# Moving the sixteen-bit split of a transposed tile from ScalarE to VectorE, and sharing its joining between the two

## The chip, the cores and the metric

The kernel runs on one core of a Trainium2 chip. The metric is the device time of one execution in microseconds. The core's engines run side by side, each with its own instruction stream: TensorE (PE, matmuls, its weight loads shown apart as PEld), VectorE (DVE), ScalarE (ACT), GpSimd (POOL) and SyncE (SP), whose queue issues most of the DMA. They wait for one another only through semaphores.

## The reference

One layer of a hybrid attention block over 256 tokens and 2048 features, in fp32, cut here to its steps:

```
h    = rms_norm(x, norm_gain)
proj = h @ w_in                       # 9,296 columns: q, k, v, gate of A; q, k, v, gate of B; indexer q, k, w
A    = chunked attention, 8 heads of 128, with a clipped relative-position bias
B    = attention over the top 64 keys of an indexer, 8 heads of 128, with a distance penalty
y    = concat(A * silu(gate_A), B * silu(gate_B))
x    = x + y @ w_out
out  = rms_norm(x, final_gain)
```

Both attentions end in a softmax whose probabilities are multiplied by the values. For that product TensorE needs the probabilities turned, keys on partitions and queries along the free axis. The change is about this turning.

## The kernel before, in words

**Blocks and units.** The weights stream through in blocks of 512 columns, each in 8 units of 512 KB. For every unit SP loads a raw slot; ScalarE copies it to a reduced-precision format (`split_hi`, L710); VectorE subtracts that from the raw slot (`split_lo`, L1013); TensorE runs the unit's matmuls with both parts (`feature_unit`, L486 and L490, or `unit`, L455 to L457). The ring has 4 slots. So `split_hi` of unit c waits until TensorE has finished unit c - 4, and SP's load of a slot waits until VectorE has split the one before in it. In the code `split_hi(g, c)` with c from 8 to 13 means unit c - 8 of the next block.

**Pairs of heads.** Blocks 10 to 17 bring in, beside their own columns, one pair of heads each: blocks 10 to 13 the four pairs of B (`feature_attention`), blocks 14 to 17 those of A (`gate_block`). TensorE computes a pair's scores after unit 1 of its block (`score_pair`) and its product with the values after unit 0 of the next (`value_pair`, first matmul L642). Between the two, written out by hand on each engine, among the splits of units 6 to 13:

- VectorE adds the bias, takes the maxima, and after ScalarE's exponentials (`exps`) scales the probabilities by the inverse sums (`normalise`, L1361 and L1365), then goes on with `split_lo` 6.
- ScalarE, after `split_hi` 6 and `features_low`, makes the planes (`planes_out`, L880): the fp32 probabilities, 768 words for each partition, are read as 1536 sixteen-bit numbers, all low halves written first and all high halves behind them.
- SP issues one DMA transpose of the sixteen-bit planes (`turn_planes`, L355), between its loads of units 1 and 2 of the next block.
- ScalarE, after `split_hi` 9 and (where there is a next pair) `stage_q`, joins the turned planes to words again (`pT_out`, L884), then copies 512 of the words in reduced precision to `pT_hi` (L886).
- VectorE subtracts that to give `pT_lo` (`pT_rest`, L1371), behind `split_lo` 9 and `stage_rest`. `value_pair` waits for it.

In the gate blocks VectorE also scales the gate (`gate_out`, L1402), ScalarE takes its tanh (`tanh_gate`, L920, ahead of `split_hi` 8), and VectorE multiplies (`gated`, L1411 and L1414).

**The end of the pairs.** After the last pair's `pT_out` and `split_hi` 10, ScalarE copies the gated outputs in reduced precision (`y_hi`, L950); VectorE, after `pT_rest` and `split_lo` 10, subtracts (`y_lo`, L1442). The output projection (L455) waits for one `y_lo` ahead of each unit.

Of the kernel before, what the change touches and what calls it, by code (L numbers as in the profile page):

```python
# [57 lines left out]
def hybrid_block(nc, xT, x, norm_gain, w_blocks, w_narrow, rel_bias, wo_blocks, final_gain, out):  # L58
# [4 lines left out]
    ACT = mybir.ActivationFunctionType  # L63
# [3 lines left out]
    with ExitStack() as ctx:  # L67
        def sb(name, shape, dt=f32):
            return ctx.enter_context(nc.sbuf_tensor(name, shape, dt))
# [4 lines left out]
        def sem(name):  # L74
            return ctx.enter_context(nc.semaphore(name))
# [26 lines left out]
        probs_T = sb("probs_T", [P, 2, P + T])  # L102
# [24 lines left out]
        probs = sb("probs", [P, 2, P + T])  # L127
# [96 lines left out]
        normed = sem("normed")  # L224
        planes_made = sem("planes_made")
        planes_turned = sem("planes_turned")
        words_made = sem("words_made")
        pt_hi_done = sem("pt_hi_done")
        pt_lo_done = sem("pt_lo_done")
        pv_done = sem("pv_done")  # L230
# [24 lines left out]
        def flat(t):  # L255
            return t.rearrange("p a b -> p (a b)")
# [23 lines left out]
        planes = flat(qiT[:, :, :]).bitcast(u16)[:, 0:2 * WORDS].rearrange("p (s n) -> p s n", s=2)  # L280
        planes_T = flat(qiT[:, :, :]).bitcast(u16)[:, 2 * WORDS:4 * WORDS].rearrange("p (s n) -> p s n", s=2)

        def halves(words):
            return flat(words[:, :, :]).bitcast(u16).rearrange("p (n s) -> p s n", s=2)
# [417 lines left out]
        def _(act):  # L702
            def split_hi(g, c):

                u = c % UNITS
                s = u % RING
                act.wait_ge(w_landed[s], g * (16 * UNITS // RING) + 16 * (c // RING + 1))
                if not (isinstance(g, int) and g * UNITS + c < RING):
                    act.wait_ge(mm_done, g * UNITS + (c - RING + 1))
                nc.scalar.activation(hi_slots[:, s, 0:UK * CB], w_raw[:, s, :], ACT.Copy).then_inc(hi_done, 1)  # L710
# [15 lines left out]
            def features_low(g, half, early, n=T):  # L726

                pair = half
                act.wait_ge(mm_done, g * UNITS + (4 * half + 4))
                if not (isinstance(g, int) and g == G_QI):  # L730
                    act.wait_ge(feat_out, feature_use(g, half, early) - 1)
                parts = acc[:, 2 * pair * CB:2 * pair * CB + 2 * CB].rearrange("p (f c) -> p f c", f=2)
                nc.scalar.activation(low[:, half, :, 0:n], parts[:, :, n:2 * n], ACT.Copy).then_inc(low_out, 1)  # L733
# [131 lines left out]
            def exps(pair, rated):  # L865
                for t, p in enumerate((p1, p0)):
                    act.wait_ge(max_done, 2 * pair + (t + 1))
                    for h in range(2):
                        if rated:
                            last = nc.scalar.activation(p[:, h, :], p[:, h, :], ACT.Exp, bias=neg_top[:, t, h:h + 1],  # L870
                                                        scale=q_rate[:, 1 - t:2 - t], accum_out=p_sum[:, t, h:h + 1])
                        else:
                            last = nc.scalar.activation(p[:, h, :], p[:, h, :], ACT.Exp, bias=neg_max[:, t, h:h + 1],  # L873
                                                        accum_out=p_sum[:, t, h:h + 1])
                last.then_inc(exp_done, 1)

            def planes_out(pair):

                act.wait_ge(normed, pair + 1)
                nc.scalar.activation(planes, halves(probs), ACT.Copy).then_inc(planes_made, 1)  # L880

            def pT_out(pair):
                act.wait_ge(planes_turned, 16 * pair + 16)
                nc.scalar.activation(halves(probs_T), planes_T, ACT.Copy).then_inc(words_made, 1)  # L884
                act.wait_ge(words_made, pair + 1)
                nc.scalar.activation(pT_hi.rearrange("p (h t) -> p h t", h=2), pT0,  # L886
                                     ACT.Copy).then_inc(pt_hi_done, 1)

            def output(pair):

                act.wait_ge(pv_done, pair + 1)
                nc.scalar.activation(o_flat[:, ds(pair * 2 * T, 2 * T)], aux[3][:, :], ACT.Copy,
                                     scale=0.5).then_inc(aux_read[3], 1)

            def feature_attention(g, i, q_next, k_next, keys):
                exps(i, True)
                split_hi(g, 6)
                features_low(g, 0, 0)
                planes_out(i)
                split_hi(g, 7)  # L900
                split_hi(g, 8)
                split_hi(g, 9)
                stage_q(q_next, k_next, keys)
                pT_out(i)
                split_hi(g, 10)
                features_low(g, 1, 0)
                split_hi(g, 11)
                split_hi(g, 12)
                output(i)
                split_hi(g, 13)  # L910
# [11 lines left out]
            def gate_block(g, i, q_next):  # L922
                exps(i + 4, False)
                split_hi(g, 6)
                features_low(g, 0, 0)
                planes_out(i + 4)
                split_hi(g, 7)
                tanh_gate(i, 0)
                split_hi(g, 8)
                split_hi(g, 9)  # L930
                if q_next is not None:
                    stage_q(q_next, q_next + 4, 8)
                pT_out(i + 4)
                split_hi(g, 10)
# [73 lines left out]
        def _(dve):  # L1008
            def split_lo(g, c):

                s = c % RING
                dve.wait_ge(hi_done, g * UNITS + (c + 1))
                nc.vector.tensor_tensor(lo_slots[:, s, 0:UK * CB], w_raw[:, s, :], hi_slots[:, s, 0:UK * CB].bitcast(f32),  # L1013
                                        ALU.subtract).then_inc(lo_done, 1)
# [33 lines left out]
            def qk_chunk(c):  # L1048
                return qk[:, ds(c, 1), :].rearrange("p o (f t) -> p (o f) t", f=2)
# [245 lines left out]
            def stage_rest(q_chunk, k_chunk, pair):  # L1295

                q_tile = qk[:, ds(q_chunk, 1), :].rearrange("p o (h t) -> p (o h) t", h=2)
                k_tile = qk[:, ds(k_chunk, 1), :].rearrange("p o (h t) -> p (o h) t", h=2)
                dve.wait_ge(q_staged, pair + 1)
                nc.vector.tensor_tensor(q_lo, q_tile[:, :, P:T], q_hi.bitcast(f32), ALU.subtract)  # L1300
                nc.vector.tensor_tensor(k_lo, k_tile, k_hi.bitcast(f32), ALU.subtract).then_inc(qk_rest, 1)
# [56 lines left out]
            def normalise(pair):  # L1358

                dve.wait_ge(exp_done, pair + 1)  # L1360
                nc.vector.reciprocal(flat(p_inv[:, :, :]), flat(p_sum[:, :, :])).then_inc(inv_done, 1)  # L1361
                dve.wait_ge(inv_done, pair + 1)
                for t, p in enumerate((p1, p0)):
                    for h in range(2):
                        last = nc.vector.tensor_scalar(p[:, h, :], p[:, h, :], p_inv[:, t, h:h + 1], None, ALU.mult)  # L1365
                last.then_inc(normed, 1)

            def pT_rest(pair):
                dve.wait_ge(pt_hi_done, pair + 1)
# [4 lines left out]
            def feature_attention(i, keys, q_next, k_next):  # L1374
                g = i + G_QKA
                bias_b(i)
                maxima(i, True)
                normalise(i)
                split_lo(g, 6)
                features_out(g, 0, 0, qk_chunk(2 * i), 2 * i + 13 if keys else None)  # L1380
                split_lo(g, 7)
                split_lo(g, 8)
                split_lo(g, 9)
                stage_rest(q_next, k_next, i + 1)
                pT_rest(i)
                split_lo(g, 10)
                features_out(g, 1, 0, qk_chunk(2 * i + 1), 2 * i + 14 if keys else None)
                split_lo(g, 11)
                split_lo(g, 12)
                split_lo(g, 13)  # L1390
# [25 lines left out]
            def gate_block(g, i, next_pair):  # L1416
                bias_a(i)
                maxima(i + 4, False)
                normalise(i + 4)
                split_lo(g, 6)  # L1420
                gate_out(g, i, 0)
                split_lo(g, 7)
                gated(i, 0)
                split_lo(g, 8)
                split_lo(g, 9)
                if next_pair:
                    stage_rest(i + 1, i + 5, i + 5)
                pT_rest(i + 4)
                split_lo(g, 10)
# [110 lines left out]
```

## Time and profile before

| | |
|---|---|
| median of 3 runs | 523.97 us (523.52 to 524.25) |
| profiled execution | 525.85 us |
| its span, first to last instruction | 523.8 us |
| mean granted TensorE clock | 0.998 of full speed |
| PE busy | 513.3 us (98%) |
| DVE busy | 367.5 us (70%) |
| ACT busy | 297.1 us (57%) |
| POOL busy | 30.2 us (6%) |

Times in the trace are counted from the span's start. A row of a timeline gives the start, the length, the engine, the line, the operation and its tiles; "x2" is two instructions merged into one row; brackets give the engine's idle time ahead of it and what ended it. An instruction may start a little before its forerunner on the same engine has written its last result, so the lengths of neighbours overlap by some 0.1 us. The buffers of the planes lie in a tile called `qiT`, so the rows name that tile.

### The profile page before, as it was taken

The page shows a single profiled execution, that of the slowest core. Times are in us where ns is not written, and L with a number is a line of the kernel's source. Part 1 is how long each engine was busy: PE and PEld are TensorE (multiplying, and loading weights), DVE is VectorE, ACT ScalarE, POOL GpSimd, SP SyncE. Part 2 cuts the span into 40 slices and gives each one's busy share as a digit, 9 for nine tenths or more (in the row PEclk, how much of TensorE's full clock was granted, in tenths as well). Part 3 has the DMA queues.
Part 4 walks back from the last instruction along what each step waited for, and adds up shares of the span by engine and source line. Part 5 has one row for each costly group of instructions (what it writes and reads, how often), then busy time and mean ns, then how long its engine had stood idle before and what let it go on. Part 6 is the DMA issues. An engine that isn't in the chain of part 4 may idle for free.

```text
span 523.8 us, 7967 instructions
## 1 busy us (share of the span) xinstructions
PE 513.3 (98%) x2864; PEld 449.3 (86%) x2864; DVE 367.5 (70%) x552; ACT 297.1 (57%) x411; POOL 30.2 (6%) x47
## 2 busy tenths in 40 slices
PE   8999999999999999999999999999999999999994
PEld 6989999988888888888888888888888878888883
DVE  5788876765857687776776867677878787646554
ACT  6775455444444433544866758595858685444342
POOL 1000052140500000000000000000000000000000
PEclk9999999999999999999999999999999999999999
DMA  8974689766675556563848475765657885566614
GB/s 282 350 223 161 201 258 287 218 186 198 199 240 185 177 184 219 181 195 107 254 135 272 113 242 154 232 189 169 190 161 213 297 233 186 175 202 196 203 42 160
DMA packets 87901, 105.69 MB, mean 202 GB/s; under 512 B 18080, under 2 KB 76352, under 8 KB 87616
## 3 DMA queue, kind: packets, MB, share of 16 engines
q1 hardware_dynamic: 86288, 99.83, 60.3%
q0 software_dynamic: 1296, 5.01, 3.0%
q10 hardware_dynamic: 288, 0.46, 0.3%
q8 instruction: 19, 0.31, 0.2%
q14 instruction: 10, 0.08, 0.1%
HBM read 99.24 MB, written 2.11 MB: 194 GB/s over the span
## 4 chain that ended last, share of the span: by engine, by line
PE 97%; DMA 1%; DVE 0%; issue 0%; ACT 0%; DVEq 0%; POOLq 0%
PE acc L486 39%; PE acc L490 19%; PE acc L455 8%; PE acc L457 8%; PE acc L456 8%; PE acc L506 5%; PE acc L514 3%; PE aux L516 2%; DMA gain<-norm_gain 1%; PE aux L633 1%; PE aux L642 1%; PE aux L630 0%; PE aux L631 0%; PE aux L629 0%; PE aux L647 0%; PE aux L576 0%
## 5 line engine op out<-in xcount | busy, mean ns | idle before, releaser
L1013 DVE TENSOR_TENSOR lo_slots<-raw_slots,hi_slots 128x1024 fp32r<-128x1024 f32 x166 | 205.3, 1244 | 106.1 <-ACT hi_slots L710 104.8
L486 PE MATMUL acc<-acts,hi_slots 128*128 128x512 f32 (+1 forms) x896 | 276.1, 389 | 0.0
L710 ACT ACTIVATE hi_slots<-raw_slots 128x1024 fp32r<-128x1024 f32 x166 | 174.7, 1057 | 158.2 <-PE acc L490 92.7
L490 PEld LDWEIGHTS acc<-acts,lo_slots 128*128 128x128 f32 x896 | 167.3, 188 | 34.0
L490 PE MATMUL acc<-acts,lo_slots 128*128 128x256 f32 (+1 forms) x896 | 174.1, 276 | 0.0
L486 PEld LDWEIGHTS acc<-acts,hi_slots 128*128 128x128 f32 x896 | 136.4, 189 | 0.1
L455 PE MATMUL acc<-hi_slots,acts 128*128 128x512 f32 x192 | 74.8, 390 | 1.0 <-issue 1.0
L456 PE MATMUL acc<-lo_slots,acts 128*128 128x512 f32 x192 | 74.7, 389 | 0.0
L457 PE MATMUL acc<-hi_slots,acts 128*128 128x512 f32 x192 | 74.7, 389 | 0.0
L455 PEld LDWEIGHTS acc<-hi_slots,acts 128*128 128x128 f32 x192 | 36.0, 188 | 8.5 <-issue 1.2
L457 PEld LDWEIGHTS acc<-hi_slots,acts 128*128 128x128 f32 x192 | 36.0, 188 | 7.5
L456 PEld LDWEIGHTS acc<-lo_slots,acts 128*128 128x128 f32 x192 | 36.0, 188 | 7.4
L506 PE MATMUL acc<-hi_slots,acts 128*128 128x512 f32 x64 | 18.7, 408 | 1.1 <-DVE acts L1056 1.1
L514 PE MATMUL acc<-hi_slots,acts 128*128 128x320 f32 x64 | 18.6, 315 | 0.0
L516 PE MATMUL aux<-hi_slots,acts 128*128 128x272 f32 x64 | 17.8, 288 | 0.0
L870 ACT ACTIVATE probs<-probs,neg_top,q_rate 128x256 f32<-128x256 f32 (+1 forms) x16 | 8.6, 537 | 16.0 <-DVE neg_top L1334 16.0
L733 ACT ACTIVATE low<-acc 128x512 f32<-128x512 f32 (+1 forms) x28 | 16.0, 571 | 1.2 <-PE acc L490 1.2
L447 POOL DMA_DIRECT2D qk<-x x1 | 0.5, 533 | 269.9 <-PE aux L633 269.9
L506 PEld LDWEIGHTS acc<-hi_slots,acts 128*128 128x128 f32 x64 | 12.0, 196 | 4.7 <-DVE acts L1056 2.5
L884 ACT ACTIVATE probs_T<-qiT 128x1536 uint16<-128x1536 uint16 x8 | 15.6, 1946 | 0.0
L873 ACT ACTIVATE probs<-probs,neg_max 128x256 f32<-128x256 f32 (+1 forms) x16 | 7.1, 445 | 11.8 <-DVE neg_max L1330 11.8
L977 ACT ACTIVATE t_gate<-z 128x512 f32<-128x512 f32 x8 | 5.0, 627 | 15.3 <-DVE z L1464 15.3
(175 smaller groups left out, 460.4 us busy)
## 6 DMA issues: line engine op xcount, KB each, us to landing
raw_slots<-w_blocks SPq DMA_DIRECT2D x140, 512.0 KB, 4.4
raw_slots<-wo_blocks SPq DMA_DIRECT2D x32, 512.0 KB, 3.7
raw_slots<-w_blocks SPq DMA_DIRECT2D x8, 256.0 KB, 5.0
qk<-x POOLq DMA_DIRECT2D x1, 2048.0 KB, 8.6
qk<-xT SPq DMA_DIRECT2D x7, 256.0 KB, 5.6
o<-ext_dram POOLq DMA_DIRECT2D x1, 1024.0 KB, 8.6
fgain<-final_gain POOLq DMA_DIRECT2D x1, 1024.0 KB, 7.9
out<-o SPq DMA_DIRECT2D x2, 512.0 KB, 3.0
```

The lines of the kernel that those rows point to most:

```text
L455: nc.tensor.matmul(dst, a_hi[:, k, t], hi, start=start, stop=False)
L456: nc.tensor.matmul(dst, a_hi[:, k, t], lo, start=False, stop=False)
L457: return nc.tensor.matmul(dst, a_lo[:, k, t], hi, start=False, stop=stop)
L486: nc.tensor.matmul(whole, w_hi4[:, u % RING, q, f * HD:f * HD + HD], acts[:, k, :, tokens], start=(k == 0), stop=False)
L490: last = nc.tensor.matmul(acc[:, bank:bank + n], w_lo4[:, u % RING, q, f * HD:f * HD + HD], a_hi[:, k, tokens], start=False, stop=(k == KT ...
L506: last = nc.tensor.matmul(acc[:, m * CB:m * CB + CB], a[:, k, m * P:m * P + P], w[:, p % RING, c], start=start, stop=stop)
L514: nc.tensor.matmul(acc[:, (TM + m) * CB:(TM + m) * CB + PART], a[:, k, t], w[:, p % RING, c:c + PART], start=start, stop=stop)
L516: last = nc.tensor.matmul(aux[m][:, 0:REST], a[:, k, t], w[:, p % RING, c + PART:c + WIDE], start=start, stop=stop)
L710: nc.scalar.activation(hi_slots[:, s, 0:UK * CB], w_raw[:, s, :], ACT.Copy).then_inc(hi_done, 1)
L733: nc.scalar.activation(low[:, half, :, 0:n], parts[:, :, n:2 * n], ACT.Copy).then_inc(low_out, 1)
L884: nc.scalar.activation(halves(probs_T), planes_T, ACT.Copy).then_inc(words_made, 1)
L1013: nc.vector.tensor_tensor(lo_slots[:, s, 0:UK * CB], w_raw[:, s, :], hi_slots[:, s, 0:UK * CB].bitcast(f32), ALU.subtract).then_inc(lo_don ...
```

## The change

The planes are made by VectorE at the end of `normalise`, and ScalarE's `planes_out` goes. The joining is cut in two: ScalarE writes the low halves of the words, VectorE the high halves (`high_halves`, between `split_lo` 9 and `stage_rest`). `pT_hi` waits for both. The semaphore `words_made` becomes `low_made` and `high_made`.

```
             def pT_out(pair):
                 act.wait_ge(planes_turned, 16 * pair + 16)
-                nc.scalar.activation(halves(probs_T), planes_T, ACT.Copy).then_inc(words_made, 1)
-                act.wait_ge(words_made, pair + 1)
+                nc.scalar.activation(halves(probs_T)[:, 0, :], planes_T[:, 0, :], ACT.Copy).then_inc(low_made, 1)
+                act.wait_ge(low_made, pair + 1)
+                act.wait_ge(high_made, pair + 1)
                 nc.scalar.activation(pT_hi.rearrange("p (h t) -> p h t", h=2), pT0,
                                      ACT.Copy).then_inc(pt_hi_done, 1)
...
-            def planes_out(pair):
-
-                act.wait_ge(normed, pair + 1)
-                nc.scalar.activation(planes, halves(probs), ACT.Copy).then_inc(planes_made, 1)
...
                 split_hi(g, 6)
                 features_low(g, 0, 0)
-                planes_out(i)
                 split_hi(g, 7)
...
             def normalise(pair):
...
                 last.then_inc(normed, 1)
+                dve.wait_ge(normed, pair + 1)
+                nc.vector.tensor_copy(planes, halves(probs)).then_inc(planes_made, 1)
+
+            def high_halves(pair):
+                dve.wait_ge(planes_turned, 16 * pair + 16)
+                nc.vector.tensor_copy(halves(probs_T)[:, 1, :], planes_T[:, 1, :]).then_inc(high_made, 1)
...
                 split_lo(g, 8)
                 split_lo(g, 9)
+                high_halves(i)
                 stage_rest(q_next, k_next, i + 1)
                 pT_rest(i)
```

`planes_out(i + 4)` goes from `gate_block` in the same way, and `high_halves(i + 4)` stands there after `split_lo` 9, ahead of `stage_rest`.

## Rows read from the trace of the kernel before

**Rows 1.** The page, part 1: busy us, share of the span, instructions.

```profile
PE 513.3 (98%) x2864; PEld 449.3 (86%) x2864; DVE 367.5 (70%) x552; ACT 297.1 (57%) x411; POOL 30.2 (6%) x47
```

**Rows 2.** TensorE's waits: line, releaser, us in total, times, longest.

```profile
PE acc L506 <- DVE acts L1056: 1.1, 1, 1.1
...
PE acc L455 <- issue: 1.0, 1, 1.0
```

**Rows 3.** Timeline of TensorE, 426.4 to 428.6 us.

```profile
426.62 0.40 PE L490 MATMUL acc<-acts,lo_slots 128*128 128x256 f32 x2
428.03 0.47 PE L455 MATMUL acc<-hi_slots,acts 128*128 128x512 f32 x1 [1.01 <-issue]
428.33 0.40 PE L456 MATMUL acc<-lo_slots,acts 128*128 128x512 f32 x1
```

**Rows 4.** Timeline of ScalarE, 414.9 to 427.3 us.

```profile
416.40 1.48 ACT L880 ACTIVATE qiT<-probs 128x1536 uint16<-128x1536 uint16 x1
...
418.78 0.64 ACT L920 ACTIVATE t_gate<-z 128x512 f32<-128x512 f32 x1
...
421.54 1.07 ACT L710 ACTIVATE hi_slots<-raw_slots 128x1024 fp32r<-128x1024 f32 x1 [1.18 <-PE acc L490]
422.51 1.94 ACT L884 ACTIVATE probs_T<-qiT 128x1536 uint16<-128x1536 uint16 x1
424.48 0.63 ACT L886 ACTIVATE parts_hi<-probs_T 128x512 fp32r<-128x512 f32 x1
```

**Rows 5.** Timeline of VectorE, 415 to 427.5 us.

```profile
415.27 1.01 DVE L1365 TENSOR_SCALAR probs<-probs,p_inv 128x256 f32<-128x256 f32 x4
416.20 1.22 DVE L1013 TENSOR_TENSOR lo_slots<-raw_slots,hi_slots 128x1024 fp32r<-128x1024 f32 x1
...
418.05 0.69 DVE L1402 TENSOR_TENSOR z<-z,rk 128x512 f32<-128x512 f32 x1
418.86 1.23 DVE L1013 TENSOR_TENSOR lo_slots<-raw_slots,hi_slots 128x1024 fp32r<-128x1024 f32 x1
...
421.40 2.46 DVE L1013 TENSOR_TENSOR lo_slots<-raw_slots,hi_slots 128x1024 fp32r<-128x1024 f32 x2
...
427.24 0.68 DVE L1442 TENSOR_TENSOR acts<-o,acts 128x512 fp32r<-128x512 f32 x1
```

**Rows 6.** ScalarE's groups by line and shape, 239 to 428 us.

```profile
L884 ACT ACTIVATE probs_T<-qiT 128x1536 uint16<-128x1536 uint16 x8 | 15.6, 1946 | 0.0
L880 ACT ACTIVATE qiT<-probs 128x1536 uint16<-128x1536 uint16 x8 | 11.8, 1474 | 0.0
```

**Rows 7.** VectorE's groups, 190 to 428 us: busy us, mean ns, idle before.

```profile
L1013 DVE TENSOR_TENSOR lo_slots<-raw_slots,hi_slots 128x1024 fp32r<-128x1024 f32 x80 | 97.0, 1222 | 33.2 <-ACT hi_slots L710 32.3
...
L1290 DVE COPY bias<-o 128x1024 f32<-128x1024 f32 x2 | 1.3, 687 | 0.0
```

**Rows 8.** Timeline of VectorE, 245.7 to 256 us (block 10).

```profile
245.75 0.18 DVE L1361 RECIPROCAL p_inv<-p_sum 128x4 f32<-128x4 f32 x1 [1.72 <-ACT probs L870]
245.97 1.01 DVE L1365 TENSOR_SCALAR probs<-probs,p_inv 128x256 f32<-128x256 f32 x4
246.89 1.22 DVE L1013 TENSOR_TENSOR lo_slots<-raw_slots,hi_slots 128x1024 fp32r<-128x1024 f32 x1
...
255.09 0.69 DVE L1371 TENSOR_TENSOR parts_lo<-probs_T,parts_hi 128x512 fp32r<-128x512 f32 x1 [1.15 <-ACT parts_hi L886]
```

**Rows 9.** Timeline of TensorE, 248.8 to 257.4 us: unit 6, the first value matmul.

```profile
248.94 0.63 PE L486 MATMUL acc<-acts,hi_slots 128*128 128x512 f32 x2
...
257.30 0.27 PE L642 MATMUL aux<-probs_T,v 128*128 128x128 f32 x1
```

**Rows 10.** Timeline of VectorE, 318 to 320 us: unit 6 of block 13.

```profile
318.67 1.22 DVE L1013 TENSOR_TENSOR lo_slots<-raw_slots,hi_slots 128x1024 fp32r<-128x1024 f32 x1
```

**Rows 11.** Timeline of TensorE, 322.3 to 322.9 us: unit 6 of block 13.

```profile
322.80 0.40 PE L486 MATMUL acc<-acts,hi_slots 128*128 128x512 f32 x1
```

**Rows 12.** The DMA transposes (line 355), from issue to landing.

```profile
DMA to landing us min/median/max: 3.7/3.7/4.0
```

More of the change, by code:

```diff
@@ L226, in hybrid_block @@
         planes_turned = sem("planes_turned")
-        words_made = sem("words_made")
+        low_made = sem("low_made")
+        high_made = sem("high_made")
         pt_hi_done = sem("pt_hi_done")
@@ L875, in exps @@
                 last.then_inc(exp_done, 1)
-            def planes_out(pair):
-                act.wait_ge(normed, pair + 1)
-                nc.scalar.activation(planes, halves(probs), ACT.Copy).then_inc(planes_made, 1)
             def pT_out(pair):
                 act.wait_ge(planes_turned, 16 * pair + 16)
-                nc.scalar.activation(halves(probs_T), planes_T, ACT.Copy).then_inc(words_made, 1)
-                act.wait_ge(words_made, pair + 1)
+                nc.scalar.activation(halves(probs_T)[:, 0, :], planes_T[:, 0, :], ACT.Copy).then_inc(low_made, 1)
+                act.wait_ge(low_made, pair + 1)
+                act.wait_ge(high_made, pair + 1)
                 nc.scalar.activation(pT_hi.rearrange("p (h t) -> p h t", h=2), pT0,
@@ L898, in feature_attention @@
                 features_low(g, 0, 0)
-                planes_out(i)
                 split_hi(g, 7)
@@ L925, in gate_block @@
                 features_low(g, 0, 0)
-                planes_out(i + 4)
                 split_hi(g, 7)
@@ L1366, in normalise, with high_halves @@
                 last.then_inc(normed, 1)
+                dve.wait_ge(normed, pair + 1)
+                nc.vector.tensor_copy(planes, halves(probs)).then_inc(planes_made, 1)
+            def high_halves(pair):
+                dve.wait_ge(planes_turned, 16 * pair + 16)
+                nc.vector.tensor_copy(halves(probs_T)[:, 1, :], planes_T[:, 1, :]).then_inc(high_made, 1)
             def pT_rest(pair):
@@ L1383, in feature_attention @@
                 split_lo(g, 9)
+                high_halves(i)
                 stage_rest(q_next, k_next, i + 1)
@@ L1425, in gate_block @@
                 split_lo(g, 9)
+                high_halves(i + 4)
                 if next_pair:
```

## The prediction

> **What bounds the kernel now.** I read the page first: TensorE is busy for 98% of the span, VectorE for 70%, ScalarE for 57%, and the chain that ended last is TensorE for 97% [rows 1]. No engine but TensorE can lengthen or shorten the time, unless it makes TensorE wait or ends a wait of it. So the second view is the list of TensorE's waits. It holds one of 1.0 us at line 455, the first matmul of the output projection, and two of 1.1 us in the first microseconds, of which one is shown [rows 2]. While the eight pairs of heads are worked on, which is where the change lies, TensorE never waits until that one at the end. So the change can gain 1.0 us at most, and it costs nothing unless VectorE or ScalarE comes late by more than its lead.
>
> The third view is the timeline around that wait [rows 3, 4, 5], read backwards. TensorE stops at 426.62 + 0.40 = 427.02 and starts at 428.03. It is released by the first `y_lo` on VectorE (427.24 + 0.68 = 427.92), so from VectorE's end to a first matmul takes 0.11. That `y_lo` stands behind `split_lo` 10, which waits for `split_hi` 10 on ScalarE, which stands behind `pT_hi` (L886, 424.48), which follows the joining of the words (L884, 422.51 + 1.94 = 424.45). The joining itself starts when `split_hi` 9 is through, and that one waited 1.18 for TensorE. So the last pair's joining is on the path that sets the end, and the seven other pairs' are not.
>
> **What the change does to the two copies.** Per pair it takes the split into planes from ScalarE (1474 ns, L880) and halves the joining there (1946 ns, L884) [rows 6]. It adds to VectorE a copy of 1536 sixteen-bit elements right behind the normalising, ahead of `split_lo` 6, and a copy of 768 ahead of `stage_rest`. Eight pairs, so 16 instructions. ScalarE's saved 1.47 + about 0.9 a pair buys nothing by itself, because ScalarE's next `split_hi` waits for TensorE to free a slot [rows 4].
>
> No row shows VectorE copying sixteen-bit elements, or with a stride of one element. The nearest is the COPY of 1024 fp32 elements, SBUF to SBUF, in 687 ns, against 1222 for a two-input instruction on as many [rows 7]. 1222 - 687 = 535 ns, about half a nanosecond for each element, so the copy runs at two elements a cycle with some 153 ns fixed (687 - 1024 x 0.521). The planes would then take 153 + 1536 x 0.521 = 954 ns, and the half 153 + 768 x 0.521 = 553. At one element a cycle they would take 1753 and 953. Writing with a stride costs something on ScalarE: L884 writes in steps and takes 472 ns longer than L880, which reads in steps; that is 0.31 ns an element, or 0.24 us on 768 elements. I take half of it for VectorE, since two elements go out together. So I use 0.95 for the planes (between 0.95 and 1.75) and 0.67 for the half (between 0.55 and 1.19).
>
> The Trainium skill speaks twice about the mode. "VectorE: DVE Perf Modes", section "Mode 1× (REGULAR) — the baseline", counts odd strides among what falls to one result a cycle; section "What auto-detection actually checks" of the same page asks for two a cycle only that one source and the destination lie in SBUF with suitable outer counts. The COPY above reads each row backwards and still runs at two a cycle, which agrees with the second. By the first section the change would cost what the first rival below costs.
>
> **Where VectorE's added time lands.** There are two places.
>
> *Place A, the first pair.* Normalising ends at 245.97 + 1.01 = 246.98, and `split_lo` 6 starts at 246.89 and ends at 248.11; TensorE takes up that unit at 248.94 [rows 8, 9]. Less the 0.11 of handing over, the lead is 0.72. VectorE comes late here because it has the distance work of the top keys in front of the first pair. With the change, the copy waits for the normalising to be written (0.04, as between 245.75 + 0.18 and 245.97), runs from 247.02 to 247.97, and `split_lo` 6, which starts 0.09 before the end of its forerunner, ends at 249.10. TensorE can start at 249.21, late by 0.27. Its first matmul after a gap holds it for 0.30 (428.03 to 428.33) against 0.23 in the stream (0.63 for two less 0.40 for one [rows 9, 11]), so 0.34 in all. Nothing gives that back later, since the whole rest of the pairs is paced by TensorE.
>
> *The pairs between.* The tightest lead of unit 6 in the seven other blocks is in the fourth: `split_lo` ends at 318.67 + 1.22 = 319.89, and TensorE takes it at 322.80 [rows 10, 11]. Less 0.11 that is 2.80, against 0.99 added (1.79 at one element a cycle). Hidden. In the first pair VectorE sat idle 1.15 ahead of `pT_rest`, waiting for ScalarE, and `pT_rest` ends at 255.09 + 0.69 = 255.78, while the first value matmuls come at 257.30 [rows 8, 9]. The added 0.95 + 0.67 fits into that idle time and that lead (1.15 + 1.52) even if nothing else absorbs it, so line 642 does not wait. The transposes land 3.7 to 4.0 after issue [rows 12]; the planes are ready no later than before (417.27 in the last pair, where ScalarE ended them at 416.40 + 1.48 = 417.88), so SP's loads behind each transpose are not held up.
>
> *Place B, the last pair.* From 415.27 to 423.86 VectorE has no gap worth the name [rows 5], so what is added moves its queue. The copy runs from 416.32 to 417.27 and everything behind it starts 0.99 later. `split_lo` 7 had waited for ScalarE (418.74 to 418.86); it now follows at once, and the shift shrinks to 0.80. `tanh` on ScalarE moves with VectorE's gate, to 419.77, and `split_hi` 8 behind it ends near 421.4 (0.64 and 1.07, less the overlap), still in time for `split_lo` 8 at 422.20. `split_lo` 9 had waited for `split_hi` 9 (422.61) and now doesn't: shift 0.70, end 424.56. The high half runs from 424.48 to 425.15. ScalarE has had the low half since about 423.6 (422.51 and a little over half of 1.94) and waits; I allow 0.10 for a hand-over with two waits, so `pT_hi` starts at 425.25 in place of 424.48. Behind it stand `split_hi` 10, `split_lo` 10, `y_hi`, `y_lo`, and TensorE, all of them moved by 0.77. The joining in two halves is faster as such; it is later because the second half queues behind two `split_lo` on the busier engine.
>
> The Trainium skill has a rule against this change: "Perfetto Trace Analysis", section "Optimizing Scalar/DVE Operations", advises moving work from a saturated VectorE to ScalarE. VectorE's 70% against 57% agrees with that direction, and place B shows it at its sharpest.
>
> **Sum.** 0.34 + 0.77 = 1.11 us. The profiled execution took 525.85 with a span of 523.8; it would take 526.96. The median of the runs is 523.97, 1.88 below that execution; the same addition makes 525.08. A measurement of this kernel tells about 0.2% (1.05 us) from no change, so the forecast stands just on the slower side of that line.
>
> **Rivals.**
> - *One element a cycle on VectorE.* For it: no sixteen-bit, strided copy in the trace. Against it: the COPY row. Place A: `split_lo` 6 ends at 249.90, TensorE 250.01, 1.07 + 0.07 = 1.14. Place B: 0.80 more for the planes and 0.28 for the half (0.95), or 0.52 (1.19): 1.85 to 2.09. Sum 2.99 to 3.23, time 527.0 to 527.2. Chance 0.18, with the case that only the half is slow (525.4 to 525.6).
> - *Hidden after all.* The leads hold: the copy starts sooner or costs less than I make it, and ScalarE's relief feeds VectorE earlier at both places. For it: ahead of 80 `split_lo` from 190 us on VectorE is idle for 33.2 us, nearly all of it waiting for ScalarE [rows 7]. Against it: none of that idle time lies between the normalising and `split_lo` 9 of the last pair. Time 523.97 to 524.4. Chance 0.18.
> - *Faster.* The one wait of TensorE shrinks: the joining in two halves lets `pT_hi` start before 424.48. It decides where the two copies on VectorE together take under about 0.85 us: 423.86 - 0.08 + half + planes - 0.25 must lie before 424.38. Here 0.25 is the 0.29 of waits given back above less the 0.04. At two elements a cycle they take 1.50 to 1.62. At four a cycle they would take 0.55 + 0.35, and it would be even. With nothing but the fixed 0.31 it would gain 0.54: 523.4. Chance 0.06.
>
> **How the numbers follow.** The forecast itself, 524.5 to 525.7, has 0.58, and some 0.37 of that lies above 525.02. Slower: 0.37 + 0.18 = 0.55. Same: 0.21 + 0.18 = 0.39. Faster: 0.06. The range goes from 524.1, which leaves out faster and the best of the hidden cases, to 527.0, which takes in the cheaper end of one element a cycle.
>
> **What would show it.** The planes' COPY on VectorE at 0.95 and the half at 0.55 to 0.7; new waits of TensorE of some 0.3 at line 486 near 249; the wait at line 455 grown from 1.0 to about 1.8; no wait at line 642. The prediction is wrong if the copies run near 1.75 and 0.95, if `split_lo` 6 of the first pair is handed over in time, or if `pT_hi` of the last pair no longer waits for the high half.

## The result, and the profile after

The changed kernel takes 525.49 us (median of 7 runs, 525.04 to 525.97) against 523.97 (7 runs, 523.52 to 524.59): a ratio of 1.0029 [1.002, 1.0038], slower by 1.52 us, with 1.05 to 1.99 inside the interval. The forecast was 525.1, slower.

Its profiled execution took 525.04 with a span of 523.0. That is less than the 525.85 and 523.8 of the execution shown of before, and says nothing of the change: the normalising of the first pair, ahead of all that was changed, lies at 243.45 where it lay at 245.97 [rows 8], 2.52 earlier, and all of that has come about in the first 10 us. A second profiled execution of the changed kernel has the same instruction at 244.09. So the two traces are compared stage by stage, and the totals by the medians of many runs. The 2.52 is called the lead below: a time of the kernel after, with the lead added, can be laid beside the times of before ("on the old scale").

The page of the kernel after, part 1 (busy us, share of the span, instructions):

```profile
PE 511.8 (98%) x2864; PEld 448.0 (86%) x2864; DVE 378.1 (72%) x568; ACT 280.0 (54%) x403; POOL 31.5 (6%) x47
```

Against [rows 1], ScalarE does 17 us less, VectorE 11 us more, and TensorE is the bound as before. The kernel after, groups by line and shape:

```profile
L1363 DVE COPY qiT<-probs 128x1536 uint16<-128x1536 uint16 x8 | 7.7, 961 | 0.3
L1367 DVE COPY probs_T<-qiT 128x768 uint16<-128x768 uint16 x8 | 4.9, 608 | 0.0
L880 ACT ACTIVATE probs_T<-qiT 128x768 uint16<-128x768 uint16 x8 | 8.5, 1068 | 0.5 <-DMA qiT<-qiT 0.5
```

The planes cost VectorE 961 ns, the high half 608, and the low half still costs ScalarE 1068. TensorE's waits after (line, releaser, us in total, times, longest):

```profile
PE acc L456 <- issue: 1.7, 1, 1.7
PE acc L498 <- DVE probs_T L1046: 1.1, 1, 1.1
PE acc L507 <- DVE acts L1051: 0.4, 1, 0.4
```

The wait at the output projection has grown from 1.0 [rows 2] to 1.7; the two others lie in the first microseconds. The page after, part 5, the weight loads of the high parts (their idle time and what ended it stand last), has a new wait, of 0.3 for `split_lo`:

```profile
L487 PEld LDWEIGHTS acc<-acts,hi_slots 128*128 128x128 f32 x896 | 136.4, 189 | 0.3 <-DVE lo_slots L1008 0.3
```

**Place A, the first pair.** VectorE in block 10 after:

```profile
243.45 1.01 DVE L1360 TENSOR_SCALAR probs<-probs,p_inv 128x256 f32<-128x256 f32 x4
244.49 0.96 DVE L1363 COPY qiT<-probs 128x1536 uint16<-128x1536 uint16 x1
245.37 1.22 DVE L1008 TENSOR_TENSOR lo_slots<-raw_slots,hi_slots 128x1024 fp32r<-128x1024 f32 x1
```

TensorE after, unit 6 of the same block:

```profile
246.19 0.40 PE L491 MATMUL acc<-acts,lo_slots 128*128 128x256 f32 x2
246.64 0.73 PE L487 MATMUL acc<-acts,hi_slots 128*128 128x512 f32 x2
```

The copy puts `split_lo` 6 off to 246.59, and TensorE starts on the unit at 246.64. With the lead of 2.52 it would have started at 248.94 - 2.52 = 246.42 [rows 9]. It is late by 0.22, and its first two matmuls take 0.73 in place of 0.63 [rows 9]: 0.32. From there to the last pair the two traces run in step: in each of the seven blocks between, the time from one unit to the next differs by 0.00 from what it was.

**Place B, the last pair.** VectorE, ScalarE and TensorE after, in that order:

```profile
414.12 0.96 DVE L1363 COPY qiT<-probs 128x1536 uint16<-128x1536 uint16 x1
...
420.00 2.36 DVE L1008 TENSOR_TENSOR lo_slots<-raw_slots,hi_slots 128x1024 fp32r<-128x1024 f32 x2
422.27 0.61 DVE L1367 COPY probs_T<-qiT 128x768 uint16<-128x768 uint16 x1
```

```profile
417.58 0.63 ACT L916 ACTIVATE t_gate<-z 128x512 f32<-128x512 f32 x1 [2.32 <-DVE z L1404]
...
420.31 1.08 ACT L880 ACTIVATE probs_T<-qiT 128x768 uint16<-128x768 uint16 x1
422.98 0.63 ACT L883 ACTIVATE parts_hi<-probs_T 128x512 fp32r<-128x512 f32 x1 [1.59 <-DVE probs_T L1367]
```

```profile
424.43 0.40 PE L491 MATMUL acc<-acts,lo_slots 128*128 128x256 f32 x2
426.53 0.47 PE L456 MATMUL acc<-hi_slots,acts 128*128 128x512 f32 x1 [1.70 <-issue]
```

Read it backwards. TensorE stands for 1.70 in place of 1.01 [rows 3]. ScalarE has written its low half at 421.39 and then stands for 1.59 until VectorE has written the high one, which queued behind two `split_lo`. The lead here is 426.62 - 424.43 = 2.19 [rows 3] (2.52 less the 0.33 lost at place A), so `pT_hi` lies at 422.98 + 2.19 = 425.17 on the old scale, against 424.48 [rows 4]: later by 0.69.

**A third place, at the very end.** The DMA view of the last microseconds, after (515 to 523 us; the row GB/s is the stretch in 40 equal slices):

```profile
GB/s 389 410 348 492 184 0 0 0 0 0 0 0 0 0 0 0 0 287 389 369 394 410 397 384 389 348 382 358 366 420 307 39 8 8 23 8 0 0 0 0
...
q14 instruction: 1, 0.01, 0.2%
...
out<-o SPq DMA_DIRECT2D x1, 192.0 KB, 4.1
```

And before (516 to 523.8 us):

```profile
GB/s 357 441 378 399 441 378 399 84 0 0 0 0 0 0 0 0 0 0 0 0 315 347 399 402 394 420 373 378 378 355 368 376 378 378 118 0 0 0 0 0
...
out<-o SPq DMA_DIRECT2D x1, 192.0 KB, 3.4
```

The last store of the result lands after 4.1 us in place of 3.4. Its burst ends as before, but a thin tail of 8 to 39 GB/s follows it, and an instruction load of 0.01 MB (one packet of 8,192 bytes, 1.1 us before the last packet of the store) on queue q14 falls into the same stretch; before has none there. From the last block's start to the end of the span the kernel after takes 0.72 longer, and nothing in the prediction speaks of that.

### The profile page after: what moved, and what is told of

Same layout as the page of the kernel before. It is cut to its first block, busy times and chain, and to the rows that moved or that the text cites. A ratio compares the mean times of both kernels' runs of the same rounds, so it can differ in the third digit from the quotient of the medians.

```text
span 523.0 us, 7985 instructions
## 1 busy us (share of the span) xinstructions
PE 511.8 (98%) x2864; PEld 448.0 (86%) x2864; DVE 378.1 (72%) x568; ACT 280.0 (54%) x403; POOL 31.5 (6%) x47
## 4 chain that ended last, share of the span: by engine, by line
PE 51%; DVE 1%; issue 1%; ACT 0%; DVEq 0%; ACTq 0%
PE acc L487 21%; PE acc L491 10%; PE acc L456 6%; PE acc L458 6%; PE acc L457 6%; PE aux L643 1%; PE aux L634 1%; PE aux L649 0%; PE aux L648 0%; PE aux L650 0%; PE aux L632 0%; PE aux L631 0%; PE aux L630 0%; ACT probs L871 0%; DVE lo_slots L1008 0%
## 5 line engine op out<-in xcount | busy, mean ns | idle before, releaser
L456 PEld LDWEIGHTS acc<-hi_slots,acts 128*128 128x128 f32 x192 | 36.0, 188 | 9.2 <-issue 1.9
L458 PEld LDWEIGHTS acc<-hi_slots,acts 128*128 128x128 f32 x192 | 36.0, 188 | 7.6
L507 PEld LDWEIGHTS acc<-hi_slots,acts 128*128 128x128 f32 x64 | 11.5, 188 | 3.6 <-DVE acts L1051 1.3
L515 PEld LDWEIGHTS acc<-hi_slots,acts 128*128 128x128 f32 x64 | 12.0, 188 | 0.3
```

The lines of the kernel that those rows point to most:

```text
L456: nc.tensor.matmul(dst, a_hi[:, k, t], hi, start=start, stop=False)
L458: return nc.tensor.matmul(dst, a_lo[:, k, t], hi, start=False, stop=stop)
L507: last = nc.tensor.matmul(acc[:, m * CB:m * CB + CB], a[:, k, m * P:m * P + P], w[:, p % RING, c], start=start, stop=stop)
L515: nc.tensor.matmul(acc[:, (TM + m) * CB:(TM + m) * CB + PART], a[:, k, t], w[:, p % RING, c:c + PART], start=start, stop=stop)
```

## The experiments

Each kernel was timed beside the kernel before; the last, contig, ran once. The table puts the times beside the traces. A and B are how much later than before TensorE comes out of the two places (the start of the unit behind each, less that of the unit ahead of it); "store" is the landing time of the last store; "places" is A + B + what the span's end lost behind the last block.

| kernel | median us (runs) | before beside it (runs) | ratio | A | B | store | places |
|---|---|---|---|---|---|---|---|
| after | 525.49 (7) | 523.97 (7) | 1.0029 [1.002, 1.0038] | 0.33 | 0.69 | 4.1 | 1.74 |
| planes_only | 524.94 (12) | 524.11 (35) | 1.0011 [0.9998, 1.0024] | 0.33 | 0.01 | 3.4 | 0.34 |
| join_only | 523.97 (12) | 524.11 (35) | 0.9997 [0.9984, 1.0011] | 0.00 | -0.01 | 3.4 | -0.02 |
| copy_late | 525.33 (12) | 524.11 (35) | 1.003 [1.0014, 1.0046] | 0.00 | 0.74 | 4.1 | 1.47 |
| no_ab | 524.87 (12) | 524.11 (35) | 1.001 [0.9997, 1.0023] | 0.00 | 1.24 | 3.4 | 1.24 |
| high_early | 524.44 (11) | 524.01 (25) | 1.0007 [0.9996, 1.0017] | 0.33 | -0.45 | 4.1 | 0.60 |
| y_first_after | 524.07 (11) | 524.01 (25) | 0.9999 [0.999, 1.0008] | 0.35 | -0.81 | 4.1 | 0.26 |
| y_first_before | 522.71 (9) | 524.01 (25) | 0.9975 [0.9965, 0.9985] | 0.00 | -0.22 | 3.4 | -0.22 |
| after_again | 525.74 (5) | 524.01 (25) | 1.0035 [1.0021, 1.0048] | 0.35 | 0.68 | 4.1 | 1.77 |
| pad_after | 525.03 (12) | 524.16 (29) | 1.0015 [1.0005, 1.0024] | 0.35 | 0.68 | 3.4 | 1.02 |
| pad_before | 524.83 (12) | 524.16 (29) | 1.0018 [1.0006, 1.003] | 0.00 | 0.00 | 4.1 | 0.72 |
| both_undone | 524.20 (12) | 524.16 (29) | 1.0002 [0.9992, 1.0012] | 0.00 | 0.01 | 3.4 | 0.01 |
| contig | 525.47 (1) | 524.16 (29) | | 0.35 | 0.43 | 4.1 | 1.51 |

**planes_only: the planes on VectorE, all the joining on ScalarE.** Against the kernel after:

```
-                nc.scalar.activation(halves(probs_T)[:, 0, :], planes_T[:, 0, :], ACT.Copy).then_inc(low_made, 1)
+                nc.scalar.activation(halves(probs_T), planes_T, ACT.Copy).then_inc(low_made, 1)
                 act.wait_ge(low_made, pair + 1)
-                act.wait_ge(high_made, pair + 1)
...
                 split_lo(g, 9)
-                high_halves(i)
...
```

In `gate_block`, `high_halves(i + 4)` goes in the same way.

> One part of the change alone: VectorE makes the planes, ScalarE joins all the words as before. Theory (two places, A in the first pair and B in the last): TensorE loses 0.33 us at unit 6 of block 10, as in the changed kernel; at the end of the pairs VectorE's 0.70 fits into the 1.28 that it sat idle ahead of pT_rest, so the wait at the output projection stays at 1.0. Sum +0.33, about 524.3. Rival 1 (the planes in VectorE's queue are the whole of place B): the wait grows to 1.7, about 525.0. Rival 2 (the loss is not at the pairs, but in the start, the last stores or the added instructions): about half of the 1.5, whatever the two places show.

In the trace place A stays, 0.33, and place B is gone: TensorE's wait at the output projection is 1.0 again. The medians show more than the 0.3 that was expected: 0.83, with -0.10 to 1.26 inside the interval, which is what the second rival gave. Part of the answer lies outside the instructions. The median span, first to last instruction, is 522.45 against 522.1, longer by 0.35 as in the trace; but what the device time holds over the span is 2.49 in the median of these executions and 2.07 in those of before. In this trace an instruction load on q14 starts 2.3 after the span has ended. That it makes the difference is not shown: join_only has one 1.8 after its span, and holds 2.09 over it.

**join_only: the joining shared, the planes on ScalarE as before.** Against the kernel after:

```
                 features_low(g, 0, 0)
+                planes_out(i)
...
                 last.then_inc(normed, 1)
-                dve.wait_ge(normed, pair + 1)
-                nc.vector.tensor_copy(planes, halves(probs)).then_inc(planes_made, 1)
...
```

`planes_out` itself comes back on ScalarE, and `planes_out(i + 4)` in `gate_block`.

> The other part alone: ScalarE makes the planes as before, the joining is shared. Theory: nothing ahead of split_lo 6, so nothing at place A; in the last pair the high half runs from about 423.8 to 424.4 (times of the kernel before) into VectorE's idle time, pT_hi starts where it did, the wait at the output projection stays at 1.0. Sum 0.0, about 524.0, so that the two parts together cost more than the sum of each alone. Rival 1 (the high half on VectorE costs its 0.61 whatever stands ahead of it): wait 1.6, about 524.6. Rival 2 (added instructions): about half of the 1.5.

No place costs anything, and no time can be told from before. So in the traces the parts do not add up: 0.34 and -0.02 alone, and 0.33 + 0.69 together. Each alone leaves place B as it was. Without the planes VectorE is through with `split_lo` 9 at 423.86 [rows 5], and 0.61 for the high half with the overlap of 0.08 ends at 424.39, just in time for `pT_hi` at 424.48 [rows 4]. ScalarE in join_only:

```profile
421.97 0.63 ACT L888 ACTIVATE parts_hi<-probs_T 128x512 fp32r<-128x512 f32 x1 [0.90 <-DVE probs_T L1372]
```

The lead of that trace is 2.51, so `pT_hi` starts at 424.48 on the old scale, where it was. ScalarE waits 0.90 for VectorE: all that the shorter joining saved it. There was no room left, and that nothing was lost is by the fall of the numbers. Without the half, `pT_hi` does not wait for VectorE at all. Only both together put the half behind a queue that the planes have already made late.

**copy_late: the planes behind `split_lo` 6.** Against the kernel after:

```
                 normalise(i)
                 split_lo(g, 6)
+                planes_out(i)
...
```

`planes_out` is cut off from the end of `normalise`; `planes_out(i + 4)` stands in `gate_block` in the same place.

> The changed kernel with the planes made behind split_lo 6 instead of ahead of it. Theory: place A is gone, place B is as it was (the same work ahead of the high half), so TensorE loses 0.69 and the time is about 524.7; the planes are ready about 1.1 later, and the transposes still land before ScalarE comes to the low half in the last pair. Rival (a later transpose takes the place of the wait removed): a wait at line 643, or place B over 0.69 by what the transposes are late. Rival 2 (not at the pairs): 525.5, as the changed kernel.

Place A is gone, and with it nothing else: TensorE's wait at the output projection is 1.8 and B is 0.74. The time, 1.22 over before where 0.7 was expected, holds the late store as well. Where the copy stands in VectorE's queue decides A, and doesn't matter to B, since either way it stands ahead of the half.

**no_ab: as copy_late, and the last pair joined by ScalarE alone.** Against copy_late:

```
+                if isinstance(pair, int) and pair == HEADS - 1:
+                    nc.scalar.activation(halves(probs_T), planes_T, ACT.Copy).then_inc(low_made, 1)
+                    act.wait_ge(low_made, pair + 1)
...
-                high_halves(i + 4)
+                if next_pair:
+                    high_halves(i + 4)
```

> As copy_late, and in the last pair ScalarE joins all the words alone. Fifteen of the sixteen added copies stay. Theory: both places are gone, TensorE's wait at the output projection is 1.0 as before and there is none at unit 6: 524.0, no change against the kernel before. Rival 2 (the loss over the 1.0 us that the two places show, or all of it, comes with the copies, the added instructions or the start): 524.5 to 525.5.

This missed. The profiled execution was the longest of the twelve (526.82). ScalarE and TensorE in it, around the output projection's start:

```profile
424.44 1.06 ACT L711 ACTIVATE hi_slots<-raw_slots 128x1024 fp32r<-128x1024 f32 x1 [1.12 <-DMA raw_slots<-wo_blocks]
```

```profile
427.46 0.77 PE L456 MATMUL acc<-hi_slots,acts 128*128 128x512 f32 x1 [2.25 <-issue]
428.02 0.63 PE L457 MATMUL acc<-lo_slots,acts 128*128 128x512 f32 x1
...
430.57 0.40 PE L457 MATMUL acc<-lo_slots,acts 128*128 128x512 f32 x1
```

Its stretches (us, busy time of each engine, granted clock, DMA share, GB/s):

```profile
424.00:427.00 3.00, 1.21 (x8) 0.86 (x6) 1.51 (x3) 2.56 (x5) 0.00 (x0) 1.00 0.64 209
428.00:430.00 2.00, 2.00 (x6) 1.61 (x5) 1.97 (x4) 2.00 (x4) 0.00 (x0) 0.50 0.65 223
```

`pT_hi` was released in time, but `split_hi` 10 waited 1.12 for its slot's load, TensorE stopped for 2.25, and then its matmuls took 0.63 in place of 0.39 to 0.40 for some 2.5 us at a granted clock of 0.50, the lower of its two levels, 1.2 GHz. That cost a further 1.42, which the table's "places" leave out. The load stands behind the last transpose in SP's queue, but SP issued it only 0.1 later than in copy_late, counted from the start of its block. Why it landed late in this execution is open, and so is why the median lies 0.76 above before; neither is a measure of place B.

**both_undone: places A and B undone in another way.** The planes go behind `split_lo` 6 only in B's four blocks, so that in the last pair they are made as early as in the kernel after, and the last pair is joined by ScalarE alone. Against no_ab:

```
                 maxima(i + 4, False)
                 normalise(i + 4)
+                planes_out(i + 4)
                 split_lo(g, 6)
-                planes_out(i + 4)
```

> The changed kernel with the planes behind split_lo 6 in the four blocks of B only, and the words of the last pair joined by ScalarE alone. Unlike no_ab it keeps the planes, and so the last transpose and the loads behind it in SP's queue, at the changed kernel's time. Theory: no wait at unit 6, the wait at the output projection is 1.0 as in the kernel before, no late load ahead of split_hi 10; the last store lands at 3.4, as it did in no_ab with the same number of instructions: 524.0. Rival (the planes on VectorE make the loads behind the last transpose late in any case): a wait over 1.0 with split_hi 10 waiting for its load, 524.5 or more.

Both places are gone, the store lands in 3.4, and the time is that of before: 1.0002. The 15 copies that VectorE still makes, eight of planes and seven of high halves, cost nothing that can be measured (the interval holds -0.4 to 0.6 us).

**high_early: the high half ahead of `split_lo` 9.** Against the kernel after, in both kinds of block:

```
-                split_lo(g, 9)
                 high_halves(i)
+                split_lo(g, 9)
```

> The changed kernel with the high half joined ahead of split_lo 9 instead of behind it. Theory (place B is the high half's place in VectorE's queue): place A stays at +0.33; in the last pair the high half ends some 1.1 earlier, pT_hi starts about 0.45 before its time in the kernel before, and TensorE's wait at the output projection falls to about 0.55, below the 1.0 of before. Sum about -0.1, time 524.0 to 524.5. Rival (the halved joining costs what it costs): wait 1.7 as in the changed kernel, 525.5.

TensorE's wait at the output projection falls to 0.6, below the 1.0 of before:

```profile
422.20 0.64 ACT L883 ACTIVATE parts_hi<-probs_T 128x512 fp32r<-128x512 f32 x1 [0.45 <-DVE probs_T L1367]
```

ScalarE waits 0.45 for the half in place of 1.59. B turns from +0.69 to -0.45: the queue ahead of the half made place B, and without it the joining in two halves is a gain. That gain is eaten by A and by the last store.

**y_first_after and y_first_before: the first `y` ahead of unit 10 of the last pair.** The same edit on both kernels:

```
             gate_block(G_OUT - 1, 3, None)
             y_hi(0)
+            split_hi(G_OUT - 1, 10)
...
             gate_block(G_OUT - 1, 3, False)
-            for q in range(4):
+            y_lo(0)
+            split_lo(G_OUT - 1, 10)
+            for q in range(1, 4):
```

`split_hi` 10 and `split_lo` 10 are left out of the last gate block in return.

> The changed kernel; in the last pair the first y_hi and y_lo stand ahead of split_hi 10 and split_lo 10. Theory: the output projection then waits for pT_hi and pT_rest alone, its wait falls from 1.7 to about 0.2, place A stays at +0.33: about 0.5 less than the kernel before, 523.5. It also takes the load behind split_hi 10 off the path. Rival (some 0.5 us of the change's cost comes with the planes on VectorE and is at neither place): about 524.0.

> The kernel before with the same reorder of the first y_hi and y_lo. Theory: pT_rest ends at 425.84, the first y_lo at about 426.5, before TensorE is through with block 17 (427.02), so the 1.0 us wait goes and nothing comes in its place: about -1.2 with the refilling of TensorE, time 522.8. Rival (something else is late next: split_hi 10 and its load, value_pair, or the next y_lo): a wait at line 455, 457 or 642 in its place, time 523.5 to 524.

TensorE in y_first_after:

```profile
425.03 0.47 PE L456 MATMUL acc<-hi_slots,acts 128*128 128x512 f32 x1 [0.21 <-issue]
```

On the kernel after, the wait of 1.70 shrinks to 0.21, and the time comes back to that of before (0.9999), though A and the late store are still in it. The time is the rival's 524.0 and not the 523.5 expected; what is left over belongs to the late store, 0.72 in this trace too, which the expectation did not hold. On the kernel before, the time falls to 522.71, a ratio of 0.9975: this beats both kernels, without the change. Its one trace shows a gain of 0.22 only. It is of the longest of its nine executions (524.62), in which `split_hi` 9 waited for its slot's load:

```profile
421.18 1.06 ACT L710 ACTIVATE hi_slots<-raw_slots 128x1024 fp32r<-128x1024 f32 x1 [1.80 <-DMA raw_slots<-wo_blocks]
```

In the trace of before that instruction waited 1.18 for TensorE [rows 4]. The medians say 1.30, with 0.79 to 1.83 inside the interval. That the other executions gain the whole wait of 1.0 fits this, but was not traced.

**after_again** is the kernel after once more.

> The changed kernel itself, again, for a second trace and more timed runs. Theory: the two places again at 0.33 and 0.69; timed median between +1.0 and +1.5. What the timed runs show over 1.02 is then looked for in the start and in the last store, where two traces can be compared.

A 0.35, B 0.68, the store at 4.1: the three places repeat. The median lies 1.73 over before, above the 1.0 to 1.5 expected and close to the 1.77 of the trace.

**pad_after and pad_before: the program's length.** 24 one-column memsets, into a spare tile, at the start of VectorE's program in the kernel after, 12 in the kernel before:

```
+            for n in range(24):
+                nc.vector.memset(spare[:, n:n + 1], 0.0)
```

> The changed kernel with 24 one-column memsets added on VectorE at its start, where it waits for the first load. Theory for the 0.72 us that the last store takes longer (an 8 KB load of instructions falls into the last store, and is VectorE's next block, reached with the change's added instructions): the load moves ahead of the stores, the last store lands 3.4 after issue as in the kernel before, and the sum falls from about 1.5 to 1.0: about 525.0. The two places stay at 0.33 and 0.69. Rival (the longer store belongs to another engine's instructions, or to the copies themselves): the store lands at 4.1 again, 525.5 to 525.7.

> The kernel before with 12 such memsets at the same place, as many as the change adds to VectorE's program text. Theory: the load of instructions falls into the last store as in the changed kernel, the store lands at about 4.1, nothing else moves: about +0.7, 524.7. Rival (VectorE's program length has nothing to do with it): 3.4, no change, 524.0.

The DMA view of the last microseconds (515 to 523 us), pad_before:

```profile
GB/s 369 21 0 0 0 0 0 0 0 0 0 0 0 123 369 379 392 382 410 397 376 369 379 379 353 369 402 154 8 15 8 23 0 0 0 0 0 0 0 0
...
q14 instruction: 1, 0.01, 0.2%
...
out<-o SPq DMA_DIRECT2D x1, 192.0 KB, 4.1
```

And pad_after:

```profile
GB/s 410 389 430 410 389 369 21 0 0 0 0 0 0 0 0 0 0 0 123 379 369 392 382 410 410 369 369 405 369 379 369 376 146 0 0 0 0 0 0 0
...
out<-o SPq DMA_DIRECT2D x1, 192.0 KB, 3.4
```

Twelve instructions that do nothing for the result bring the thin tail, the instruction load and the 4.1 to the kernel before, and 0.67 us by the medians. Twenty-four more take all three away from the kernel after, whose excess falls from 1.52 to 0.87. So the third place belongs to the number of instructions in VectorE's program, and not to what they do. The times of the loads on q14 show the same. From 30 us to the end the kernel after has eleven. In pad_after five of them come earlier: those at 39.0, 170.9, 242.0, 348.3 and 521.0 lie at 31.5, 143.2, 237.5, 336.2 and 476.8. The six others stay within 0.6 us. Only VectorE's program was padded, so those five bring its instructions, and the one that fell into the store is among them. The spare tile by itself doesn't take the load away: contig, below, has a larger one and no padding, and its store lands in 4.1.

**contig: the high half written without a stride.** It goes to a spare tile, so the words keep the high halves of what stood there before; that part of the joining is left out. Against the kernel after:

```
+        spare = sb("spare", [P, WORDS], u16)
...
-                nc.vector.tensor_copy(halves(probs_T)[:, 1, :], planes_T[:, 1, :]).then_inc(high_made, 1)
+                nc.vector.tensor_copy(spare[:, :], planes_T[:, 1, :]).then_inc(high_made, 1)
```

> The changed kernel in which VectorE's copy of the high halves writes 768 neighbouring numbers of a spare tile in place of every second one of the words, so the words keep old high halves. Theory (two elements a cycle, and writing in steps costs VectorE little): 0.55 against the 0.61 of the changed kernel, place B smaller by 0.06. Rival (one element a cycle with the step, two or four without): 0.35.

```profile
L1369 DVE COPY spare<-qiT 128x768 uint16<-128x768 uint16 x8 | 2.8, 352 | 0.0
```

The time of the rival came, 0.35, and not the 0.55 of the theory: 352 ns in place of 608, further down than two elements a cycle allow by the prediction's own line (153 + 768 x 0.521 = 553). B falls by the same 0.26, from 0.69 to 0.43: what the half costs VectorE goes into the last pair one for one.

## Why the prediction was right

**What bounds it.** Right. TensorE is busy for 98% before and after. ScalarE's 17 us less bought no time in any of the blocks with a pair.

**The price of the copies.** 0.95 predicted, 0.961 measured for the planes; 0.67 predicted, 0.608 for the half. The first rival, one element a cycle (1.75 and 0.95), falls with that. But the way to the 0.67 was wrong. It took two elements a cycle for what a plain copy would do and added half of ScalarE's price for a stride. Contig shows that the plain sixteen-bit copy takes 352: with the prediction's fixed 153 that is 0.26 ns an element, four elements a cycle. The stride of the destination costs 256 ns, not 120, and brings it to 0.59 ns, a little slower than two a cycle. The planes, which are read with a stride, come to 0.53, two a cycle. The Trainium skill, "VectorE: DVE Perf Modes", section "What auto-detection actually checks", says as much: the highest mode needs one source and the destination in SBUF and also sixteen-bit elements that lie next to one another; the first alone gives two a cycle. 352 agrees with the highest mode and 961 with two a cycle; 608 lies 55 above two a cycle by the line above. One result a cycle for odd strides, which the prediction set beside it, fits none of the three. The prediction's two errors on the half, the pace and the price of the stride, nearly cancelled, to 0.06; that is luck.

**Place A.** 0.34 predicted; 0.33 in the trace, 0.33 to 0.35 in every kernel that keeps the copy ahead of `split_lo` 6, 0.00 in the others. On the old scale (2.52 added) the copy was to run from 247.02 to 247.97 and `split_lo` 6 to end at 249.10; they show 247.01, 247.97 and 249.11. Behind that two small terms were off and nearly cancelled: the hand-over to TensorE took 0.05 (246.59 to 246.64) in place of 0.11, and the first two matmuls held it for 0.10 more than in the stream in place of 0.07.

**The pairs between.** Right: 0.00 in each of seven blocks, and no wait at the value product.

**Place B.** 0.77 predicted, 0.69 measured. The steps, on the old scale (2.19 added): `tanh` at 419.77 (predicted 419.77), `split_lo` 8 at 422.19 (422.20), the high half at 424.46 (424.48), the hand-over to ScalarE 422.98 - 422.88 = 0.10 (0.10), `pT_hi` at 425.17 (425.25). Of the 0.08 that are missing, 0.06 are the half's shorter time and 0.02 its earlier start. That the half is late because of the queue ahead of it, and not because of the joining in two, is shown by high_early (-0.45) and join_only (0.00).

**The sum.** 1.11 predicted, 0.33 + 0.69 = 1.02 in the trace, and 1.52 by the medians. The prediction came out on the right side with a part of the time that its sum does not hold: the last store, 0.72 in the trace, 0.67 by pad_before's medians. That part is luck. The term that failed is one that the prediction set at nothing without saying so, the length of VectorE's program. With it the three places make 1.74, inside the 1.05 to 1.99 of the measurement; without it (pad_after) 1.02, with 0.87 by the medians. By its own two places alone the change would stand at the line between slower and no change, where the prediction put it.

**The other rivals.** Hidden after all: no, the leads at both places fell short as worked out. Faster: not as written. But high_early, y_first_after and contig show its condition to be the right one: what `pT_hi` or the first `y_lo` waits for in the last pair decides, and an order that lets the half go first takes 0.45 off the wait.

## What to carry to other kernels

Where two edits load the same engine, price them together at each place where that engine's queue ends a wait: here, in the traces, the parts cost 0.34 and nothing alone, and 1.02 together, because the second stood in the queue that the first had made late. The order around the one wait of the bounding engine was worth more than the choice of engine: one instruction on each of two engines, moved ahead of one split, gained 1.30 us on the kernel before, where the change lost 1.52. And before a fraction of a per cent is put down to what an edit does, pad the program with idle instructions: twelve of them moved the kernel before by 0.7 us.

## What the runs showed of the hardware that was not expected

- An instruction load on q14 that falls into the last store puts its landing off from 3.4 to 4.1 us, in all seven traces in which it does, and in none of the seven others. The Trainium skill, "Runtime: NRT & Kernel Launch", section "Instruction fetch mechanics", says that an engine's sequencer fetches its program in blocks over a DMA queue of its own, at a cost that is mostly hidden. Here it is not: the kernel ends with the wait for that store. By pad_after the load is one of VectorE's. In four of the other seven traces it comes only after the span's end, and in three there is none behind 502 us.
- Sixteen-bit copies on VectorE: 768 elements in 352 ns without a stride, 608 with a stride in the destination. With a stride in the source VectorE takes 961 for 1536. On ScalarE the strided half takes 1068.
- After a stop of 2.25 us (no_ab) TensorE ran at a granted clock of 0.50, 1.2 GHz, for some 2.5 us, and lost 1.42 us; after stops of 1.70 (after) and 1.75 (copy_late) the matmuls took 0.39 to 0.40 from the second on. Three of copy_late's twelve executions took 527.2 to 527.8, against a median of 525.33; that they are of this kind was not traced.
